# A two-model feed-forward kernel on one core: GpSimd's order around the seven-product steps, turned inner sums in two parts, and x rounded before it is squared

## What is computed

```python
def _swiglu(h, w_gate, w_up, w_down):
    return (silu(h @ w_gate) * (h @ w_up)) @ w_down

x = x + MACARON * _swiglu(_rmsnorm(x, ffn1_norm), ffn1_w_gate, ffn1_w_up, ffn1_w_down)
...
x = x + swiglu(rms_norm(x, ffn_norm[layer]), ffn_w_gate_up[layer], ffn_w_down[layer])
```

## Time and profile before

| | |
|---|---|
| median of 3 executions | 3320.42 us (3320.33 to 3321.43) |
| the profiled execution, its own time | 3321.34 us |
| span in the profile, first to last instruction | 3320.0 us |
| TensorE (PE) busy | 3158.0 us, 95% |
| VectorE (DVE) busy | 2236.7 us, 67% |
| ScalarE (ACT) busy | 1613.2 us, 49% |
| GpSimd (POOL) busy | 1704.7 us, 51% |
| mean granted TensorE clock | 0.981 of full speed |

### The profile page before, as it was taken

One profiled execution on the slowest core, in us unless ns is written; L12 is line 12 of the kernel. 1 busy time (PEld: TensorE's weight loads), 2 busy tenths in 40 slices (PEclk: granted clock), 3 DMA queues, 4 the chain that ended last, 5 costly groups with the idle time before them and its releaser, 6 DMA issues. The chain is left out here.

```text
span 3320.0 us, 52492 instructions
## 1 busy us (share of the span) xinstructions
PE 3158.0 (95%) x20424; PEld 2877.0 (87%) x20424; DVE 2236.7 (67%) x2975; ACT 1613.2 (49%) x2525; POOL 1704.7 (51%) x952
## 2 busy tenths in 40 slices
PE   9999999999999989999998999999989999999999
PEld 7989888898979989887898877888989788889998
DVE  7767467876667765477776577458766686477764
ACT  5445433544545444434544455545444475454443
POOL 5666533666647566434656543226566212256664
PEclk9999999999999999999999999999999999999999
DMA  4222322222222222322222232322222223322222
GB/s 141 90 100 105 119 77 83 96 90 102 103 88 90 103 102 95 120 83 76 90 102 98 84 102 77 121 89 96 90 100 104 92 90 126 102 89 90 102 102 77
DMA packets 93318, 322.60 MB, mean 97 GB/s; under 512 B 10512, under 2 KB 14992, under 8 KB 93072
## 3 DMA queue, kind: packets, MB, share of 16 engines
q1 hardware_dynamic: 87680, 312.07, 27.2%
q10 hardware_dynamic: 5392, 7.17, 0.7%
HBM read 316.05 MB, written 2.10 MB: 96 GB/s over the span
## 5 line engine op out<-in xcount | busy, mean ns | idle before, releaser
L3065 POOL TENSOR_TENSOR wlo<-raws,whi 128x1024 fp32r<-128x1024 f32 x369 | 954.0, 2590 | 893.4 <-ACT whi L1188 893.1
L1188 ACT ACTIVATE whi<-raws 128x1024 fp32r<-128x1024 f32 x422 | 441.3, 1052 | 129.0 <-PE bank L481 57.2
L3062 POOL TENSOR_TENSOR f_sl<-raws,f_sh 128x512 fp32r<-128x512 f32 x166 | 215.5, 1298 | 387.0 <-ACT f_sh L1308 387.0
L616 PE MATMUL bank<-gxh,whi 128*128 128x256 f32 x1064 | 275.8, 290 | 16.3 <-ACT acc L1323 16.2
L1294 ACT ACTIVATE whi<-banks 128x1024 fp32r<-128x1024 f32 (+1 forms) x166 | 165.1, 995 | 258.3 <-DVE banks L2162 205.7
L617 PE MATMUL bank<-gxl,whi 128*128 128x256 f32 x1064 | 270.2, 284 | 0.0
L2157 DVE TENSOR_TENSOR banks<-raws 128x1024 f32<-128x1024 f32 (+1 forms) x166 | 268.0, 1614 | 0.0
L616 PE MATMUL bank<-f_th,f_sh 128*128 128x256 f32 x944 | 246.3, 292 | 13.3 <-DVE bank L2183 13.3
L617 PE MATMUL bank<-f_tl,f_sh 128*128 128x256 f32 x944 | 244.4, 290 | 0.0
L477 PE MATMUL bank<-gxh,whi 128*128 128x512 f32 x584 | 230.4, 394 | 11.7 <-DVE gxl L2109 11.7
L2236 DVE TENSOR_TENSOR f_u<-bank,f_s 128x512 f32<-128x512 f32 x132 | 91.2, 691 | 222.7 <-issue 188.4
(11 more groups left out here) (590 smaller groups left out, 9277.8 us busy)
## 6 DMA issues: line engine op xcount, KB each, us to landing
raws<-stream SPq DMA_DIRECT2D x588, 512.0 KB, 3.4
xa_mem<-memT ACTq DMA_DIRECT2D x2, 1024.0 KB, 6.2
m_dk<-decay ACTq DMA_DIRECT2D x2, 514.0 KB, 4.5
x<-xT ACTq DMA_DIRECT2D x4, 256.0 KB, 5.3
x<-xT SPq DMA_DIRECT2D x4, 256.0 KB, 6.7
outT<-x SPq DMA_DIRECT2D x2, 512.0 KB, 3.0
m_ct<-cos ACTq DMA_DIRECT2D x2, 256.0 KB, 2.7
m_sn<-sin ACTq DMA_DIRECT2D x2, 256.0 KB, 3.0
```

What stands on the lines that cost most here:

```text
L616: pe.matmul(out, seq(hi, k, P), moving[k][0], start=first and k == 0, stop=False, skip_group_check=n != 1)
L1188: act.activation(M.whi[r][:, :], M.raw[r][:, :], ACT.Copy).then_inc(*S.tick("hi", u))
L3062: pool.tensor_tensor(seq(T[f"sl{s % 2}"], 0), seq(M.raw[r], 1), seq(T[f"sh{s % 2}"], 0).bitcast(F32), ALU.subtract).then_inc(*S.tick("lo", u))
L3065: pool.tensor_tensor(M.wlo[r][:, :], M.raw[r][:, :], M.whi[r][:, :].bitcast(F32), ALU.subtract).then_inc(*S.tick("lo", u))
```

## The change

Three things are reordered, and the turned hidden parts are made in two pieces.

1. GpSimd in a step (`pool_program`): before it makes the first unit's low part it waits for the first weight sum of VectorE (`s13`). The second unit's low part moves behind `scale` and behind the two `part`s of a down step.
2. Turned hidden parts. The first quarter needs the even tile alone: its high and low part are now made at the even tile (256 columns), the other three quarters at the odd tile (768 columns). For odd tiles other than 7 and 13 below 14 (`turned_late`) that work moves behind `c22`, into the next step, on all three engines. In the first down step of a block, product 5 waits for the first pieces and product 6 for the rest.
3. Order of a down step: TensorE does product 2 before product 6 (`sixth`), ScalarE does `snap5` before `s13_hi`.
4. `residual`: ScalarE makes `gxh` before the square, `turn_hi` and `turn_lo` move to the front of an even tile, and GpSimd's low part of output unit m waits for the sum of squares of tile m-3 (`BEHIND`).

```diff
+BEHIND = {residual_units(i)[0] + m: (i, m - 3) for i in range(12) if i != M2_STAGE
+          for m in range(X_EARLY + 1, KD if i == F_STAGE[5] else KD + 2)}
...
+def turned_late(f, s):
+
+    m = (SEQS[f][s - 1] if s else ("tile", PLAIN[f] - 1))[1] if s >= 0 and (not s or SEQS[f][s - 1][0] == "tile") else 0
+    return m if m % 2 and m < PAIRED and m + 1 not in (F_PARTS[0][1], F_PARTS[1][1]) else 0
...
-                arrive = {1: [("hidden", f, 2 * p) for p in ps], 5: [("turned_h_lo", f, p) for p in ps],
-                              2: [("hidden", f, 2 * p + 1) for p in ps]}
+                    arrive = {1: [("hidden", f, 2 * p) for p in ps], 5: [("turned_h_lo_first", f, p) for p in ps],
+                              2: [("hidden", f, 2 * p + 1) for p in ps], 6: [("turned_h_lo", f, p) for p in ps]}
...
             product(2, s, (seq(M.whi[first], 1), seq(M.wlo[first], 1)), up_lo, y[:, 0:HALF], False, arrive.get(2))
+            if item[0] == "down":
+                sixth(s, x, arrive.get(6))
...
             act.wait_ge(*S.at("xs", i, m))
+            if i < F_STAGE[5]:
+                act.activation(seq(M.gxh, m), seq(M.x, m), ACT.Copy, scale=gain(m)).then_inc(*S.tick("gxh", i, m))
             act.wait_ge(*S.at("acc", i, m - 1))
             act.activation(M.sq[:, :], seq(M.x, m), ACT.Square).then_inc(*S.tick("sq", i, m))
...
+            if turned_late(f, s - 1):
+                turned_hidden_hi(turned_late(f, s - 1))
             snap(1, s)
+            if SEQS[f][s][0] == "down":
+                snap(5, s)
...
             if s:
                 c22(s - 1)
+            if turned_late(f, s - 1):
+                turn_hidden(turned_late(f, s - 1))
             if after:
                 sums(s + 1)
...
         pool.wait_ge(*S.at("hi", u))
+        if u in BEHIND:
+            pool.wait_ge(*S.at("acc", *BEHIND[u]))
...
+            if s + 1 < len(SEQS[f]):
+                first, second = rows(f, s + 1)
+                pool.wait_ge(*S.at("s13", f, s + 1))
+                lo(first)
...
+            if turned_late(f, s - 1):
+                turned_hidden_lo(turned_late(f, s - 1))
             if before[0] == "tile":
                 scale(before[1])
-                hidden_lo(before[1])
             if item[0] == "down":
                 m = 2 * item[2]
                 part(s, 5, m + 1, of_half(M.x, 1, m + 1), M.acc[:, 0:HALF])
                 part(s, 6, m, seq(M.x, m), M.sq[:, :])
+            if second is not None:
+                lo(second)
+            if before[0] == "tile":
+                hidden_lo(before[1])
+                if before[1] < PAIRED and turned_late(f, s) != before[1]:
+                    turned_hidden_lo(before[1])
```

More of the change, by code:

```diff
@@ L62, with residual_units @@
 PAIRED = F_PARTS[2][0]
+def residual_units(i):
+    if i in F_STAGE:
+        return [U["down", F_STAGE.index(i), 2, m] for m in range(KD)]
+    if i in M1_STAGE:
+        return [U["o1", M1_STAGE.index(i), m] for m in range(KD)]
+    if i in XA_STAGE:
+        return [U["xo", XA_STAGE.index(i), m] for m in range(KD)]
+    return [U["o3", m] for m in range(KD)]
 def column_plan():
@@ L173 @@
     "f_vector": "s13 s13_lo s2 s4 s24_lo c1 c22 turned_parts turned_lo part_sum turned_h",
-    "f_scalar": "s13_hi s24_hi snap1 snap5 snap6 gained turned_hi hh turned_h_hi",
-    "f_pool": "silu_scaled hidden turned_h_lo part_pool",
+    "f_scalar": "s13_hi s24_hi snap1 snap5 snap6 gained turned_hi hh turned_h_hi turned_h_hi_first",
+    "f_pool": "silu_scaled hidden turned_h_lo turned_h_lo_first part_pool",
     "m1_vector": "ga ws rot_table gsum gsq centred diagonal col_rstd vsum vbias z0 ginv vn hinv ret_n ret_g y1h y1 rot_c rot_s rot_in rope gg sm "
@@ L644, in fourth, with sixth @@
             product(4, s, (seq(T[f"sh{s % 2}"], 0), seq(T[f"sl{s % 2}"], 0)), low_part(u), x[:, 0:HALF], False)
+        def sixth(s, x, arrive=None):
+            pe.wait_ge(*S.at("s24_hi", f, s))
+            pe.wait_ge(*S.at("snap1", f, s))
+            product(6, s, (seq(T[f"sh{s % 2}"], 1), seq(T[f"sl{s % 2}"], 1)), ("s24_lo", f, s), x[:, 0:HALF], False, arrive)
         def seven(s):
@@ L668, in seven @@
                 fourth(s - 1)
-            pe.wait_ge(*S.at("s24_hi", f, s))
-            pe.wait_ge(*S.at("snap1", f, s))
-            product(6, s, (seq(sh, 1), seq(sl, 1)), ("s24_lo", f, s), x[:, 0:HALF], False)
+            if item[0] == "tile":
+                sixth(s, x)
             pe.wait_ge(*S.at("snap5", f, s))
             product(2, s, (seq(M.whi[first], 1), seq(M.wlo[first], 1)), up_lo, y[:, 0:HALF], False, arrive.get(2))
+            if item[0] == "down":
+                sixth(s, x, arrive.get(6))
             product(3, s, (seq(sh, 2), seq(sl, 2)), ("s24_lo", f, s), y[:, HALF:], False)
@@ L1333, in step @@
                 s13_hi(after)
-            snap(5, s)
+            if SEQS[f][s][0] == "tile":
+                snap(5, s)
             if after is not None:
@@ L1354, in begin @@
             hidden_hi(late)
+            turned_hidden_hi(late)
         if f:
@@ L2107, in residual @@
                 continue
+            if i + 1 in F_STAGE and m and m % 2 == 0:
+                turn_lo(F_STAGE.index(i + 1), m // 2 - 1)
             dve.wait_ge(*S.at("gxh", i, m))
@@ L2123, in residual @@
                 dve.tensor_tensor(M.R[:, :], M.R[:, :], M.sd[:, :], ALU.add).then_inc(*S.tick("acc2", m))
[L2124 to L2129 removed]
+            if i + 1 in F_STAGE and m % 2:
+                turn_parts(F_STAGE.index(i + 1), m // 2)
     def fresh():
@@ L2260, in begin @@
             hidden(late)
+            turn_hidden(late)
             s24_lo(0)
@@ L2278, in step @@
                 hidden(before[1])
+                if before[1] < PAIRED and turned_late(f, s) != before[1]:
+                    turn_hidden(before[1])
             first_row(s)
```

63 lines of the change are left out of this document (40 added, 23 removed).

## The result

The changed kernel takes 3124.76 us (median of 4, 3124.11 to 3124.97) where the kernel before takes 3320.66: ratio 0.9409, 95% interval 0.9393 to 0.9426. That is 195.9 us less, where I had forecast 170.5 (3150 us, range 3112 to 3202). The forecast's own range of 3125 to 3185 missed it by 0.2 us.

What follows compares the result with a forecast made beforehand. TensorE's waits and the low clock after them were taken to lose 203.5 us of the 3320.0 us span. Gains of 54 + 64.5 + 22.5 + 19 + 10.5 = 170.5 off 3321.3 gave about 3150 us, range 3112 to 3202.

Steps and rivals of the forecast that it cites:

- Transitions: Down steps 0,0 and 1,0: turned parts in two pieces, product 6 behind 2; of 79.9 us lost, gain 54.
- what is late next: Down steps 0,0 and 1,0: `c22`, `snap6` and low clock still cost 2.0 and 2.3 us each, 26 us left.
- Other down steps: Down steps behind 0,0 and 1,0, to tile 15: earlier `snap5` and `part` gain 64.5 of 73.2 us lost.
- Tiles: Tile steps up to 8, 13 and 14: earlier `c22` and `scale` gain 22.5 of 28.1 us lost.
- rival 1: VectorE and GpSimd hold each other up in the new places: about 3219 us (3185 to 3265), chance 0.18.
- Wait for `s13`: First steps: GpSimd's first low part no longer holds up VectorE's sum; gain 19 of 22.3 us lost.
- Residual: Ahead of feed-forwards: rounding before the square cuts the 11.7 us wait for `gxl` to 1; gain 10.5 us.
- Rival 2: All steps: nothing new waits at all, 10 to 15 us lost in steps, about 3115 us; chance 0.08.

Runs made afterwards that it cites:

- u1: The changed kernel, but product 5 of the first down step waits for the whole turned low part again, not its first piece; 3173.93 us, ratio 0.9556.
- u7: The changed kernel, but product 6 stands ahead of product 2 in down steps, as in the kernel before; 3129.10 us, ratio 0.9413.
- b34: The kernel before with only GpSimd's new order: wait for `s13` ahead of the first low part, second low part behind `scale` and the additions; 3196.36 us.
- u3: The changed kernel, but GpSimd's second low part runs right behind the first again, ahead of `scale` and both parts; 3215.11 us, ratio 0.9679.
- u34: The changed kernel without GpSimd's wait for `s13` and with its second low part right behind the first again; 3311.78 us, ratio 0.9971.
- u6: The changed kernel with `turned_late` returning 0, so an odd tile's turning stands right behind its hidden tile again; 3130.77 us, ratio 0.9418.
- u4: The changed kernel without GpSimd's wait for VectorE's sum (`s13`) ahead of the first low part; 3192.91 us, ratio 0.9613.
- n1: The changed kernel, with GpSimd's low parts of the second gate and up tile in five feed-forwards also waiting for `acc_lo`; 3109.78 us, ratio 0.9363.
- u2: The changed kernel, but in down steps ScalarE's `snap5` runs behind `s13_hi` again; 3153.48 us, ratio 0.9494.
- n13: n1 plus, in step 1,0, tile 14's `scale` behind GpSimd's two additions and its hidden tile made a step later; 3114.70 us, ratio 0.9369.

## Why the prediction was right, and where its steps were not

The time came out within 25 us and its sign was right, because the sum was made by stretches: what a stretch could lose was known from windows and counts, and nearly all of it went. The causes I gave inside the stretches held less well, and that the errors of four stretches nearly cancel is luck: the first steps gave 8 us less than forecast, the tiles 4, the other down steps 1 and the residual 5 more. The transitions' 24.6 us more are what is left.

- **Transitions (predicted gain 54, measured 78.6).** Right in mechanism: u1 gives back 49 us by product 5 alone. The step that failed is "what is late next": I had added 0.3 to 0.8 us for `c22`, 1 us for `snap6` and rests of low clock, 2.0 and 2.3 us a transition. They measured 0.15 us, nothing and nothing. The late `snap6` was priced as if VectorE's sums stayed where they were. Product 6 behind 2 is worth little (u7). This term is as large as the whole difference between 3150 and 3125.
- **Other down steps (64.5 predicted, 65.5 measured).** The size is right, the reason is so in part only. I put most of it on `snap5` and down 1,1 on `part`; b34 keeps `snap5` late and loses 1.4 us there. GpSimd's order was the cause: the second low part's place by itself (u3 loses 25 us more there), both edits together (u34, 50). `snap5`'s place becomes worth 28 us only with product 2 ahead of product 6.
- **Tiles (22.5 predicted, 26.1 measured).** GpSimd's `scale` was named, rightly (u3), but with 0.5 us a step. `c22` ahead of the turning, the other cause named, is worth little in the new kernel (u6, 6.6 us in the tiles). (The 21.7 us of the two-tile loop is also a little high: 362.69 us for 17 pairs are 21.3, 129.06 for six 21.5.) That the low part would fall on the turning operations was held in rival 1, and the `s13` wait, which excludes just this, was priced in another place.
- **Wait for `s13` (19 predicted in first steps, 11.0 measured there).** The cause is right for the kernel before: with GpSimd's order alone (b34) the sum stands still nowhere in the first steps, and they lose 12.5 us less. What failed is to take this as what the wait does in the new kernel. Without it the first steps are unchanged (u4), since the halves part the two instructions as well (u34), and the tiles lose 64 us more. I read L2157's 2.98 us in one first step and priced the wait there alone; the turning operations in their new place I held against GpSimd's second low part (rival 1) and not against its first. The size fell short since only four of the six first steps had the held-up sum, and since VectorE was late for a second reason, the end of the sum of squares (n1: 9 of the 11.3 us left).
- **Residual (10.5 predicted, some 15 measured outside the steps).** Undone it costs 13 us. That it would give 1 to 2 us more in first steps was wrong: it moves 5 us of waiting into them. GpSimd's wait for the sum of squares was never seen to hold TensorE up.
- **Rival 1, at 0.18,** names what happens without the `s13` wait: in u4 the turning operations are held up, and its 3193 us lie inside the rival's 3185 to 3265. That they do is luck: the rival had the transitions keep 54 us and the tiles 28, and u4 loses 2.0 and 67.1 there. The Trainium skill, "SBUF — State Buffer", "Who interferes with whom", says that a VectorE instruction with two SBUF inputs and a GpSimd one that reads SBUF exclude each other, and that the order of issue decides who waits; the rows agree (2.61 us against 0.72 with the low part 0.08 us ahead, 2.88 against 0.68). In the tile steps the change escapes it by that one wait.
- **Rival 2, at 0.08** (nothing new waits, 10 to 15 us left, 3115), is nearest to what happened: 23.7 left, of which 11.3 in first steps. Its time was added up wrongly, though: a gain of 190 + 11 us gives about 3120, not 3115.

What stays open: no run moved VectorE's turning alone in the kernel before, or undid it together with GpSimd's order, so its share of the 187 us is read from rows and not measured. Nor did a run undo `snap5`'s place and product 2's together.

## What to carry to other kernels

Sum a forecast by stretches, with window lengths against counts of work, and only then by causes: the first survived misread causes. Undo parts in pairs, and make one alone in the old kernel too: a part undone alone costs nothing where another covers for it (first steps), and its price depends on what else is changed (`snap5` late: 1.4 us left in b34, where product 2 stands behind 6, 28 us in u2, where it stands ahead). A stretch that loses nothing with a part left old doesn't make the part needless in the new order: look at when its result is due in each. Where two engines hold each other up, read the changed order of both engines side by side, since a wait that puts one behind the other can be worth more than every removed stall (68 us here, 187 with its neighbour), and an instruction moved on one engine alone can cost what it saves together. Before an instruction is moved later, list all that wait for it, readers of its bank too (n13).

## What the runs showed of the hardware

- VectorE operations with two inputs in SBUF waited out a GpSimd instruction that was already running in all rows looked at: 2.61 us in place of 0.72 (u4), 2.60 in place of 0.41 (u34), 2.88 and 2.70 in place of 0.68 (after). A lead of 0.08 us decided it. In the other direction GpSimd's turned low part grew from 1.85 (u34) to 2.82 us (after), and the pair of low parts at 2770.99 is 5.66 us where 2 x 2.41 would be 4.82.
- A wait of 3.4 us on TensorE cost about 5 us of its stretch (u1, step 0,0), with the granted clock at 0.79 to 0.89 for it; waits of 1.0 us (down 1,1 after, which loses 1.2 us) left it at 1.00. Between them the price varied: in step 1,0 of u1 TensorE waits 2.7 us in each of the six feed-forwards, and the step loses 2.9 us where the clock stayed at 1.00 (twice) and 4.4 to 5.6 where it was 0.75 to 0.86.
